# Sixty-four prompt tokens instead of 32 left out of the dense expert products, and two waits moved

## The chip, the cores and the metric

The kernel runs on one core of one Trainium2 chip. The metric is the device time of one execution in microseconds (us). Engines are named as in the profile: PE is TensorE (PEld its weight loads), DVE is VectorE, ACT is ScalarE, POOL is GpSimd, and SP is the engine that only issues DMAs here.

## What is computed

One inference step of a decoder layer, for a prompt of 512 tokens and for 8 sampled tokens, 1024 wide. After an attention and mLSTM part, whose code the change does not touch, comes a layer of single-neuron experts (PEER). Each token has 8 heads, and each head picks 16 of 128 x 128 = 16384 experts:

```python
e = i1[ci // 16] * 128 + i2[ci % 16]              # 8 heads x 16 = 128 experts of each token
g = softmax(sc)                                    # their weights
a = gelu(einsum('td,ted->te', hb, u[e]))           # one dot product for each token and expert
out = einsum('te,ted->td', g * a, v[e])            # weighed sum of the rows of v
```

## The kernel before

The picks are spread over all experts, so the kernel computes most of the layer densely.

**First phase.** For each of 128 chunks of 128 experts (`n` in the code; the table `u` is loaded in groups `g` of four chunks), PE multiplies the table by all 520 tokens: `up(n)`, 32 matmuls of 260 columns (line 2129). Two PSUM pairs alternate, and `up(n)` waits for `gelu(n - 2)` of ACT. ACT applies gelu into `act_f` (line 989) and splits the loaded `u_raw` into `u_g` (line 980); DVE makes the remainder `u_a` (line 1549). SP loads `u` two groups ahead (line 573), and stores the results to HBM: `d_act` for the tokens of the dense part (line 579), `d_acts` for the rest (line 581). Beside the chunks, from n = 45 on, one pair of gates a step turns the picks of 8 dense tokens into dense gate weights: DVE makes one-hot rows, PE multiplies them (line 2150, 16 matmuls), ACT moves them into `stage` (line 997), and SP stores a filled `stage` to `d_gate` (line 585) after every fourth pair. There are NPAIRS pairs.

**Second phase.** For each of the 128 chunks (`q`), PE multiplies the table `v` by the activations times gates: 16 matmuls of DENSE columns (line 2181), the product of a high part (`v_g`, `w_h`) and of a remainder (`v_a`, `w_y`). For each group SP loads `a_in` and `g_in` (`load_weighing`, lines 597 and 598, after DVE has used up the group two before) and 2 MB of `v_raw` (`load_v`, line 591, after PE is done with the group three before). For each chunk ACT makes `v_g` (line 1010) and `w_h` (line 1024), DVE makes `v_a` (line 1722), `w_y` (line 1728) and `w_grown` (line 1715). They may be up to 8 chunks ahead of PE.

**Left out of the dense part.** The last EXTRA prompt tokens and the 8 sampled ones are handled by slots. A slot is 128 pairs of token and expert, one on each partition. POOL gathers one number of `d_acts` for each (`t_dots`, line 792) and one row of `v` of 4 KB for each (`trow`, line 798, 6 buffers, so six slots ahead); DVE weighs four slots' numbers (line 1745) and adds each row times its weight (lines 1749 and 1752) into `s_acc` (sampled tokens, first 8 slots) or `x_acc`. At the end PE sums over the partitions of a token (line 2199). The function `slots_at(q)` says behind which chunk q DVE does which slot, in its own queue, so that a row that has not come holds up DVE.

**The seam of the phases.** The first group of the second phase is prepared while PE is still in the first. SP, in its loop over n, waits at n = AT_FIRST until all gate stores have landed, and then issues the loads of group 0; these and the `u` loads are in one queue. At n = AT_PREPARE and the three steps behind it ACT and DVE prepare its chunks.

Of the kernel before, what the change touches and what calls it, by code (L numbers as in the profile page):

```python
# [34 lines left out]
NG = NKEYS // GC  # L35
TB = 32
LATER = SEQ - P
EXTRA = 32
DENSE = SEQ - EXTRA
NBLK = DENSE // TB  # L40
QUADS = TB // 4
# [6 lines left out]
SSLOTS = DB * H * TOPK // P  # L48
TSLOTS = SSLOTS + EXTRA * H * TOPK // P
BATCH = 4  # L50
LEAD = 6
DOTS = 4
KEPT = EXTRA + DB
SPREAD = P // EXTRA
assert H % SPREAD == 0 and TSLOTS % BATCH == 0 and DENSE % TB == 0
# [7 lines left out]

def slots_at(q):

    return [s for s in range(TSLOTS) if 8 + s * 29 // 10 == q]


COLT = 32
# [5 lines left out]
AT_EXP = 31  # L75
AT_TABLES = 34
AT_GATES = 45
AT_FIRST = 106
AT_PREPARE = 112


def gate_pairs_at(n):
# [78 lines left out]
def trunk_and_peer(nc, I, O):  # L161
# [37 lines left out]
    def put(name, shape, dt, off):  # L199
        return nc.alloc_sbuf_tensor_at(name, shape, dt, offset=off)  # L200
# [23 lines left out]
    t_who = put("t_who", [P, 1], F32, c0 + 4928 + 20 * TSLOTS)  # L224
    xsel = put("xsel", [P, EXTRA], F32, c0 + 8064)
    ones_row = put("ones_row", [H, SEQ], F32, c0)
# [271 lines left out]
    with nc.allow_non_contiguous_dma(reason="a few hundred small elements of the decode batch"), block as blk:  # L498

        @blk.sync  # L500
        def _(sp):
# [81 lines left out]
            def store_gates(n):  # L583
                sp.wait_ge(gl_ev, (n + 1) * QUADS)
                sp.dma_start(d_gate[:, :, GC * TB * n:GC * TB * (n + 1)].rearrange("g p x -> p g x"),
                             stage[n % 2][:, :, :].rearrange("p (g c) t -> p g (c t)", c=GC)).then_inc(g_stored[n % 2], 16)
# [18 lines left out]
            for n in range(NKEYS):  # L605
# [8 lines left out]
                for pair in gate_pairs_at(n):  # L614
                    if pair % (QUADS // 2) == QUADS // 2 - 1:
                        store_gates(pair // (QUADS // 2))
                if n == AT_FIRST:
                    for b in range(2):
# [17 lines left out]
        def _(pool):  # L636
# [146 lines left out]
            for h in range(H):  # L783
                at, s0 = EXTRA * (h % SPREAD), SSLOTS + h // SPREAD * TOPK
                pool.dma_start(t_lists[at:at + EXTRA, :, s0:s0 + TOPK],
# [27 lines left out]
        def _(act):  # L813
# [161 lines left out]
            def u_shrunk(g, s):  # L975
                act.wait_ge(u_in[g % 2][s // 2], 16 * (g // 2 + 1))
                if g >= 2:
                    act.wait_ge(a_made, (g - 1) * GC)
                ks = slice(2 * s, 2 * s + 2)
                A(u_g[g % 2][s // 2][:, 2 * (s % 2):2 * (s % 2) + 2, :], u_raw[g % 2][:, ks, :], ACT.Copy, scale=SHRINK  # L980
                  ).then_inc(ug_done, 1)
# [18 lines left out]
            def v_shrunk(q):  # L1000
                g, c = q // GC, q % GC
                if c == 0:
                    act.wait_ge(v_in[g % VRING], 16 * (g // VRING + 1))
                if q == 0:
                    act.wait_ge(gl_mm, NQUADS)
                if q == GC:
                    act.wait_ge(a_made, NKEYS)
                if q >= VGRING:
                    act.wait_ge(down_used, q - VGRING + 1)
                A(v_g[q % VGRING][:, :], v_raw[g % VRING][:, c, :], ACT.Copy, scale=SHRINK).then_inc(vg_done, 1)  # L1010

            def weights_high(q):
                g, c = q // GC, q % GC
                act.wait_ge(w_made, q + 1)
                if q == 0:
                    for b in range(2):
                        act.wait_ge(g_stored[b], 16 * ((NBLK + 1 - b) // 2))
                if q == GC:
                    for b in range(2):
                        act.wait_ge(a_stored[b], 16 * (NG // 2))  # L1020
                        act.wait_ge(as_stored[b], 16 * (NG // 2))
                if q >= WRING:
                    act.wait_ge(down_used, q - WRING + 1)
                A(w_h[g % 2][:, c, :], w_grown[q % 3][:, :], ACT.Copy, scale=1.0 / GROW).then_inc(wh_done, 1)  # L1024
# [24 lines left out]
            for n in range(NKEYS):  # L1049
# [9 lines left out]
                if n % GC < 2 and 1 <= n // GC < NG - 1:  # L1059
                    for s in (2 * (n % GC), 2 * (n % GC) + 1):  # L1060
                        u_shrunk(n // GC + 1, s)
                if 0 <= n - AT_PREPARE < GC:
                    v_shrunk(n - AT_PREPARE)
                    weights_high(n - AT_PREPARE)
            for q in range(GC, CHUNKS):
# [4 lines left out]
        def _(v):  # L1070
# [475 lines left out]
            def u_rest(g, s):  # L1546
                v.wait_ge(ug_done, g * 4 + s + 1)
                ks = slice(2 * s, 2 * s + 2)
                tt(u_a[g % 2][:, ks, :], u_raw[g % 2][:, ks, :],  # L1549
                   u_g[g % 2][s // 2][:, 2 * (s % 2):2 * (s % 2) + 2, :].bitcast(F32), ALU.subtract).then_inc(ulow_done, 1)  # L1550
# [168 lines left out]
            def v_rest(q):  # L1719
                g, c = q // GC, q % GC  # L1720
                v.wait_ge(vg_done, q + 1)
                tt(v_a[g % VRING][:, c, :], v_raw[g % VRING][:, c, :], v_g[q % VGRING][:, :].bitcast(F32), ALU.subtract  # L1722
                   ).then_inc(vlow_done, 1)
# [7 lines left out]
            def down_step(q):  # L1731
                if 0 <= q - 1 < CHUNKS:
                    v_rest(q - 1)
                if 0 <= q - 2 < CHUNKS:
                    weights_rest(q - 2)
                if q < CHUNKS:
                    weights_grown(q)
# [17 lines left out]
            for n in range((FIRST_LOOPED - 1) * GC, NKEYS):  # L1755
                for pair in gate_pairs_at(n):
                    gate_rows(pair)
                if n % GC == GC - 1 and n // GC + 1 < NG:
                    for s in range(4):
                        u_rest(n // GC + 1, s)  # L1760
                if 0 <= n - AT_PREPARE < GC:
                    down_step(n - AT_PREPARE)
                if n == AT_PREPARE + GC:
                    v_rest(GC - 1)
# [5 lines left out]
            for q in range(GC + 2, CHUNKS + 2):  # L1770
                down_step(q)
                for s in slots_at(q):
                    slot_row(s)
# [538 lines left out]
```

## Time and profile before

| | us |
|---|---|
| Median of 3 runs | 1540.96 (1540.72 to 1545.38) |
| The profiled execution | 1541.64 |
| Its span, first to last instruction | 1539.7 |
| First phase on PE | 513.5 to 1079.1 |
| Second phase on PE | 1079.2 to about 1536 |

PE is busy for 98% of the span, DVE 73%, ACT 39%, POOL 23%. Of the chain of work that ended last, lines 2129 and 2181 are 29% and 28%. The DMA engines are busy 8 to 10 tenths of the time in the second phase up to about 1480 us. Times below count from the start of the span.

### The profile page before, as it was taken

Reading aid. Unit: us, or ns where it says so; the run is one execution under the profiler, and the core shown is the slowest. Engines: PE = TensorE matmul, PEld = TensorE weight load, DVE = VectorE, ACT = ScalarE, POOL = GpSimd, SP = SyncE. Lnnn points to the kernel's source line nnn. Section 1 sums busy time; section 2 is a strip of 40 time slices with the busy share of each in tenths; the row PEclk is TensorE's granted clock in tenths of the full one; section 3 lists DMA queues with packets and bytes.
Section 4 is the critical chain, followed back from the end, with each engine's and each line's share of the span. In section 5 each row is a group of like instructions: output and inputs, shape, how many; then the busy total and the mean of one; then the engine's idle time right before and its main releaser. Section 6 shows DMA issues by size and latency. Waiting matters only on the chain.

```text
span 1539.7 us, 25005 instructions
## 1 busy us (share of the span) xinstructions
PE 1507.4 (98%) x9760; PEld 1288.7 (84%) x9760; DVE 1122.4 (73%) x2475; ACT 601.2 (39%) x992; POOL 347.5 (23%) x369
## 2 busy tenths in 40 slices
PE   9999999999999999999999999979899999999999
PEld 7834445788888999999999999979788888888888
DVE  8739885674999899667777777242488877777773
ACT  2012126600233434535555555343344444444441
POOL 0100213502156576110000000000654533331000
PEclk9999999999999999999999999989999999999999
DMA  5243562404211356667888888866899999889861
GB/s 199 102 109 119 160 221 83 166 4 160 88 55 56 130 173 215 199 211 234 275 278 276 275 279 276 297 231 239 337 387 409 361 346 362 334 340 352 322 266 56
DMA packets 141717, 345.66 MB, mean 225 GB/s; under 512 B 25304, under 2 KB 103408, under 8 KB 127008
## 3 DMA queue, kind: packets, MB, share of 16 engines
q1 hardware_dynamic: 131344, 316.33, 57.8%
q0 software_dynamic: 9968, 27.66, 5.1%
q8 instruction: 78, 1.28, 0.3%
q14 instruction: 39, 0.32, 0.1%
q10 hardware_dynamic: 288, 0.07, 0.0%
HBM read 270.63 MB, written 73.35 MB: 223 GB/s over the span
## 4 chain that ended last, share of the span: by engine, by line
PE 84%; DVE 9%; DMA 4%; ACT 1%; issue 1%; POOL 1%; SPq 0%; DVEq 0%; ACTq 0%; POOLq 0%
PE psum L2129 29%; PE psum L2181 28%; PE psum L1790 20%; PE psum L2150 4%; DMA qrow<-d_q 1%; DMA u_raw<-in_uT 1%; DMA d_gate<-stage 1%; DMA trow<-in_v,t_lists 1%; PE psum L1932 1%; POOL t_dots L792 1%; PE psum L2011 1%; DVE u_a L1549 1%; PE psum L1796 0%; DVE kprod L1216 0%; PE psum L1950 0%
## 5 line engine op out<-in xcount | busy, mean ns | idle before, releaser
L2129 PE MATMUL psum<-h_h,u_g 128*128 128x260 f32 x2048 | 419.0, 286 | 12.6 <-ACT act_f L989 9.9
L2129 PE MATMUL psum<-h_y,u_a 128*128 128x260 f32 x2048 | 410.4, 282 | 0.0
L2181 PE MATMUL psum<-w_h,v_g 128*128 128x480 f32 x1024 | 390.6, 381 | 6.1 <-DVE w_y L1728 6.1
L2181 PE MATMUL psum<-w_y,v_a 128*128 128x480 f32 x1024 | 389.5, 380 | 0.0
L2129 PEld LDWEIGHTS psum<-h_h,u_g 128*128 128x128 f32 x2048 | 315.2, 189 | 13.6 <-ACT act_f L989 10.1
L2129 PEld LDWEIGHTS psum<-h_y,u_a 128*128 128x128 f32 x2048 | 316.4, 189 | 0.0
L1549 DVE TENSOR_TENSOR u_a<-u_raw,u_g 128x1024 fp32r<-128x1024 f32 x128 | 151.2, 1225 | 143.1 <-ACT u_g L980 143.1
L1722 DVE TENSOR_TENSOR v_a<-v_raw,v_g 128x1024 fp32r<-128x1024 f32 x128 | 156.2, 1220 | 99.0 <-ACT v_g L1010 99.0
L2181 PEld LDWEIGHTS psum<-w_h,v_g 128*128 128x128 f32 x1024 | 193.1, 189 | 37.0 <-DVE v_a L1722 6.4
L2181 PEld LDWEIGHTS psum<-w_y,v_a 128*128 128x128 f32 x1024 | 193.1, 189 | 30.1
L1010 ACT ACTIVATE v_g<-v_raw 128x1024 fp32r<-128x1024 f32 x128 | 134.3, 1049 | 122.3 <-DMA v_raw<-in_v 122.3
L989 ACT ACTIVATE act_f<-psum 128x520 f32<-128x520 f32 x128 | 77.4, 605 | 265.6 <-PE psum L2129 265.6
L1790 PE MATMUL psum<-hT,wr 128*128 128x260 f32 x768 | 169.9, 383 | 0.0
L1790 PEld LDWEIGHTS psum<-hT,wr 128*128 128x128 f32 x768 | 145.4, 190 | 22.4 <-DMA wr<-in_w 0.4
L792 POOL DMA_INDIRECT t_dots<-d_acts,t_lists x40 | 56.8, 1421 | 433.5 <-DMA d_acts<-act_f 421.6
L980 ACT ACTIVATE u_g<-u_raw 128x1024 fp32r<-128x1024 f32 x128 | 128.5, 1059 | 28.6 <-DMA u_raw<-in_uT 28.5
L1790 PE MATMUL psum<-wr,hT 128*128 128x512 f32 x304 | 132.4, 593 | 0.0
L798 POOL DMA_INDIRECT trow<-in_v,t_lists x40 | 85.6, 2139 | 188.8 <-DVE x_acc L1752 155.9
L1024 ACT ACTIVATE w_h<-w_grown 128x480 fp32r<-128x480 f32 x128 | 77.1, 602 | 117.7 <-DVE w_grown L1715 114.4
L1790 PEld LDWEIGHTS psum<-wr,hT 128*128 128x128 f32 x304 | 57.0, 190 | 69.3 <-issue 69.3
L1715 DVE SCALAR_TENSOR_TENSOR w_grown<-a_in,g_in 128x480 f32<-128x480 f32 x128 | 83.4, 652 | 15.6 <-DMA g_in<-d_gate 15.5
L1728 DVE SCALAR_TENSOR_TENSOR w_y<-w_h,w_grown 128x480 fp32r<-128x480 f32 x128 | 83.2, 651 | 0.0
(399 smaller groups left out, 1693.6 us busy)
## 6 DMA issues: line engine op xcount, KB each, us to landing
u_raw<-in_uT SPq DMA_DIRECT2D x64, 1024.0 KB, 7.5
v_raw<-in_v SPq DMA_DIRECT2D x32, 2048.0 KB, 8.5
d_act<-act_f SPq DMA_DIRECT2D x32, 960.0 KB, 11.4
d_gate<-stage SPq DMA_DIRECT2D x15, 2048.0 KB, 12.0
a_in<-d_act SPq DMA_DIRECT2D x32, 960.0 KB, 7.4
g_in<-d_gate SPq DMA_DIRECT2D x32, 960.0 KB, 10.1
wr<-in_w SPq DMA_DIRECT2D x13, 2048.0 KB, 8.1
kv<-in_ck SPq DMA_DIRECT2D x24, 256.0 KB, 8.3
```

The source lines that it names most:

```text
L798: pool.indirect_dma_start(trow[s % TROWS][:, :], None, v_rows, bass.IndirectOffsetOnAxis(ap=t_vrow[:, s:s + 1], axis=0)).then_inc(t_row_in ...
L980: A(u_g[g % 2][s // 2][:, 2 * (s % 2):2 * (s % 2) + 2, :], u_raw[g % 2][:, ks, :], ACT.Copy, scale=SHRINK).then_inc(ug_done, 1)
L989: A(act_f[g % 2][:, c, :], upair[n % 2], ACT.Gelu).then_inc(a_gelu, 1)
L1010: A(v_g[q % VGRING][:, :], v_raw[g % VRING][:, c, :], ACT.Copy, scale=SHRINK).then_inc(vg_done, 1)
L1024: A(w_h[g % 2][:, c, :], w_grown[q % 3][:, :], ACT.Copy, scale=1.0 / GROW).then_inc(wh_done, 1)
L1549: tt(u_a[g % 2][:, ks, :], u_raw[g % 2][:, ks, :], u_g[g % 2][s // 2][:, 2 * (s % 2):2 * (s % 2) + 2, :].bitcast(F32), ALU.subtract).then_ ...
L1715: stt(w_grown[q % 3][:, :].rearrange("p (a t) -> p a t", a=NBLK), a_in[g % 2][:, c, :].rearrange("p (a t) -> p a t", a=NBLK), GROW, g_in[g ...
L1722: tt(v_a[g % VRING][:, c, :], v_raw[g % VRING][:, c, :], v_g[q % VGRING][:, :].bitcast(F32), ALU.subtract).then_inc(vlow_done, 1)
L1728: stt(w_y[g % 2][:, c, :], w_h[g % 2][:, c, :].bitcast(F32), 1.0 - GROW, w_grown[q % 3][:, :], ALU.mult, ALU.add).then_inc(wy_done, 1)
L1790: mm = pe.matmul(dst, l, r, start=(n == 0), stop=(n == len(pairs) - 1))
L2129: mm = pe.matmul(upair[n % 2][:, cols], w, hs[:, k, cols], start=(k == 0 and x == 0), stop=(k == KT - 1 and x == 1))
L2181: mm = pe.matmul(ybank[m][:, 0:DENSE], w, z[g % 2][:, c, :], start=(q == 0 and x == 0), stop=(last and x == 1))
```

## The change

```diff
-EXTRA = 32
+EXTRA = 64
 DENSE = SEQ - EXTRA
 NBLK = DENSE // TB
 QUADS = TB // 4
...
 def slots_at(q):
-    return [s for s in range(TSLOTS) if 8 + s * 29 // 10 == q]
+    return [s for s in range(TSLOTS) if 16 + s * 3 // 2 == q]
...
-AT_FIRST = 106
-AT_PREPARE = 112
+AT_FIRST = 109
+AT_PREPARE = 115
```

Everything else follows from these numbers: DENSE goes from 480 to 448, the gate pairs from 60 to 56 and their stores from 15 to 14, the slots from 40 to 72, SPREAD (partitions a token of the prompt has in a slot) from 4 to 2, KEPT (columns of `d_acts`) from 40 to 72. Slots stood behind chunks 8 to 121, one each 2.9 chunks; now they stand behind chunks 16 to 122, two for each three chunks.

SP's queue around the loads of group 0. Before (`v_raw_250`, `a_in_264` and `g_in_266` are the buffers of group 0, the `u_raw` behind them is group 28's):

```order
L573 DMA u_raw_228<-in_uT 128x2048 x2
L579 DMA d_act<-act_f_236 512x1x480
L581 DMA d_acts<-act_f_236 128x4x40
L585 DMA d_gate<-stage_244 128x32x128
L591 DMA v_raw_250<-in_v 128x4096
L597 DMA a_in_264<-d_act 128x1920
L598 DMA g_in_266<-d_gate 128x1920
L573 DMA u_raw_227<-in_uT 128x2048 x2
```

and now:

```order
L585 DMA d_gate<-stage_245 128x32x128
L573 DMA u_raw_228<-in_uT 128x2048 x2
L579 DMA d_act<-act_f_236 512x1x448
L581 DMA d_acts<-act_f_236 128x4x72
L573 DMA u_raw_227<-in_uT 128x2048 x2
L579 DMA d_act<-act_f_235 512x1x448
L581 DMA d_acts<-act_f_235 128x4x72
L591 DMA v_raw_250<-in_v 128x4096
L597 DMA a_in_264<-d_act 128x1792
L598 DMA g_in_266<-d_gate 128x1792
L573 DMA u_raw_228<-in_uT 128x2048 x2
```

The loads of group 0 move from ahead of the `u_raw` load of group 28 to behind it, and there is a whole group between the last gate store and them.

DVE's queue around the first slot. Before, behind `w_grown` of chunk 8 (the `v_a` rows are of chunks 6, 7 and 8):

```order
L1722 TENSOR_TENSOR v_a_254<-v_raw_251,v_g_262 128x1024
L1728 SCALAR_TENSOR_TENSOR w_y_274<-w_h_272,w_grown_270 128x480
L1715 SCALAR_TENSOR_TENSOR w_grown_269<-a_in_265,g_in_267 128x480
L1722 TENSOR_TENSOR v_a_254<-v_raw_251,v_g_263 128x1024
L1728 SCALAR_TENSOR_TENSOR w_y_274<-w_h_272,w_grown_268 128x480
L1715 SCALAR_TENSOR_TENSOR w_grown_270<-a_in_264,g_in_266 128x480
L1745 TENSOR_TENSOR t_wts<-t_dots,t_lists 128x4
L1749 TENSOR_SCALAR s_acc<-trow_275,t_wts 128x1024
L1722 TENSOR_TENSOR v_a_255<-v_raw_252,v_g_256 128x1024
L1728 SCALAR_TENSOR_TENSOR w_y_274<-w_h_272,w_grown_269 128x480
```

and now, behind `w_grown` of chunk 16:

```order
L1715 SCALAR_TENSOR_TENSOR w_grown_269<-a_in_264,g_in_266 128x448
L1745 TENSOR_TENSOR t_wts<-t_dots,t_lists 128x4
L1749 TENSOR_SCALAR s_acc<-trow_275,t_wts 128x1024
L1722 TENSOR_TENSOR v_a_254<-v_raw_251,v_g_256 128x1024
L1728 SCALAR_TENSOR_TENSOR w_y_274<-w_h_272,w_grown_268 128x448
L1715 SCALAR_TENSOR_TENSOR w_grown_270<-a_in_264,g_in_266 128x448
L1752 SCALAR_TENSOR_TENSOR s_acc<-trow_276,t_wts,s_acc 128x1024
L1722 TENSOR_TENSOR v_a_254<-v_raw_251,v_g_257 128x1024
L1728 SCALAR_TENSOR_TENSOR w_y_273<-w_h_271,w_grown_269 128x448
L1715 SCALAR_TENSOR_TENSOR w_grown_268<-a_in_264,g_in_266 128x448
L1722 TENSOR_TENSOR v_a_254<-v_raw_251,v_g_258 128x1024
L1728 SCALAR_TENSOR_TENSOR w_y_273<-w_h_271,w_grown_270 128x448
```

The first slot stood ahead of the `w_y` of chunk 7 (the last row of the first piece); now it stands eight chunks further on, and the second follows after one chunk instead of after two.

## Rows read from the trace of the kernel before

**Rows 1.** The page: span, then an engine's busy time (share) and instructions.
```profile
span 1539.7 us, 25005 instructions
PE 1507.4 (98%) x9760; PEld 1288.7 (84%) x9760; DVE 1122.4 (73%) x2475; ACT 601.2 (39%) x992; POOL 347.5 (23%) x369
```
**Rows 2.** Timeline, ACT: start, duration, engine, line, operation, operands, [idle before <-releaser].
```profile
972.59 0.61 ACT L989 ACTIVATE act_f<-psum 128x520 f32<-128x520 f32 x1 [3.21 <-PE psum L2129]
...
977.39 0.60 ACT L989 ACTIVATE act_f<-psum 128x520 f32<-128x520 f32 x1 [3.21 <-PE psum L2129]
...
1071.69 0.61 ACT L989 ACTIVATE act_f<-psum 128x520 f32<-128x520 f32 x1 [3.23 <-PE psum L2129]
1075.52 0.61 ACT L989 ACTIVATE act_f<-psum 128x520 f32<-128x520 f32 x1 [3.23 <-PE psum L2129]
```
**Rows 3.** Timeline, PE, second phase, two matmuls 50 apart.
```profile
1300.04 0.37 PE L2181 MATMUL psum<-w_y,v_a 128*128 128x480 f32 x1
...
1310.92 0.38 PE L2181 MATMUL psum<-w_y,v_a 128*128 128x480 f32 x1
```
**Rows 4.** Timeline, ACT and SP, around the loads of group 0.
```profile
989.85 0.61 ACT L989 ACTIVATE act_f<-psum 128x520 f32<-128x520 f32 x1 [3.23 <-PE psum L2129]
...
990.87 0.35 SPq L591 DMA_DIRECT2D v_raw<-in_v  x1
...
992.21 1.08 SPq L573 DMA_DIRECT2D u_raw<-in_uT  x2
...
1008.64 2.00 ACT L980 ACTIVATE u_g<-u_raw 128x1024 fp32r<-128x1024 f32 x2 [14.36 <-DMA u_raw<-in_uT]
```
**Rows 5.** Timeline, PE, behind that stall; ten rows of two matmuls apart.
```profile
1011.19 0.80 PE L2129 MATMUL psum<-h_h,u_g 128*128 128x260 f32 x2 [9.88 <-ACT act_f L989]
...
1015.60 0.41 PE L2129 MATMUL psum<-h_h,u_g 128*128 128x260 f32 x2
```
**Rows 6.** Timeline, POOL and DVE, the first gathers and the first slot.
```profile
1086.00 1.06 POOL L792 DMA_INDIRECT t_dots<-d_acts,t_lists  x1 [421.57 <-DMA d_acts<-act_f]
...
1098.24 0.16 DVE L1745 TENSOR_TENSOR t_wts<-t_dots,t_lists 128x4 f32<-128x4 f32 x1 [4.52 <-DMA t_dots<-d_acts,t_lists]
1107.07 0.75 DVE L1749 TENSOR_SCALAR s_acc<-trow,t_wts 128x1024 f32<-128x1024 f32 x1 [8.66 <-DMA trow<-in_v,t_lists]
```
**Rows 7.** Timeline, PE, behind the second stall; 12 matmuls apart.
```profile
1109.67 0.74 PE L2181 MATMUL psum<-w_h,v_g 128*128 128x480 f32 x1 [6.06 <-DVE w_y L1728]
...
1114.55 0.38 PE L2181 MATMUL psum<-w_h,v_g 128*128 128x480 f32 x1
```
**Rows 8.** Timeline, DVE, working without a gap.
```profile
1112.28 1.28 DVE L1752 SCALAR_TENSOR_TENSOR s_acc<-trow,t_wts,s_acc 128x1024 f32<-128x1024 f32 x1
1113.48 1.22 DVE L1722 TENSOR_TENSOR v_a<-v_raw,v_g 128x1024 fp32r<-128x1024 f32 x1
...
1115.75 1.22 DVE L1722 TENSOR_TENSOR v_a<-v_raw,v_g 128x1024 fp32r<-128x1024 f32 x1
```
**Rows 9.** Windows: stretch, length, busy by engine, PE clock, DMA share, GB/s.
```profile
1160.00:1200.00 40.00, 40.00 (x187) 34.59 (x185) 30.53 (x40) 17.30 (x23) 14.36 (x8) 1.00 1.00 409
```
**Rows 10.** DMA queues, 1130 to 1170 us: packets, MB, share of the 16 engines.
```profile
q1 hardware_dynamic: 1453, 13.27, 82.0%
q0 software_dynamic: 880, 2.62, 16.5%
```
**Rows 11.** Timeline, SP's load of group 8, and DVE's first use of it.
```profile
1171.38 0.33 SPq L591 DMA_DIRECT2D v_raw<-in_v  x1
...
1181.87 1.23 DVE L1722 TENSOR_TENSOR v_a<-v_raw,v_g 128x1024 fp32r<-128x1024 f32 x1 [2.91 <-ACT v_g L1010]
```
**Rows 12.** Groups of POOL's instructions, 1120 to 1440 us: busy, mean ns | idle before.
```profile
L798 POOL DMA_INDIRECT trow<-in_v,t_lists x32 | 76.0, 2375 | 186.4 <-DVE x_acc L1752 155.9 <-DVE s_acc L1752 23.6 <-DVE x_acc L1749 6.0
L792 POOL DMA_INDIRECT t_dots<-d_acts,t_lists x27 | 40.7, 1508 | 8.2 <-issue 8.2
```
**Rows 13.** Timeline, POOL: one request made while DVE ran without a gap.
```profile
1206.99 7.71 POOL L792 DMA_INDIRECT t_dots<-d_acts,t_lists  x1 [0.31 <-issue]
```

## The prediction

> **What bounds the kernel now.** I read the page first: PE is busy 1507 of 1539.7 us [rows 1], so time can be gained by fewer columns on PE or by taking its few waits away, and lost by whatever supplies PE. Next come the timelines at both ends of the first phase's last part, for the pace of a step: gelu rows are 4.80 us apart where a gate pair lies in the step and 3.83 us where none does [rows 2], which is 0.1197 us for each of 32 matmuls of 260 columns. In the second phase 50 matmuls of 480 columns take 10.88 us, 0.2176 us each, 3.48 us a chunk [rows 3]. Then the waits of PE. Only two are longer than 3 us, one at the seam (9.88 us, rows 5) and one early in the second phase (6.06 us, rows 7). Last, the suppliers in the second phase: DVE [rows 8], the DMA engines [rows 9, 10] and POOL [rows 12, 13].
>
> **Fewer columns.** 2048 matmuls lose 32 of 480 columns. Between 260 and 480 columns the pace rises by 0.2176 - 0.1197 = 0.0979 us for 220 columns, 0.445 ns a column, so 14.2 ns a matmul and 29.1 us in all. In proportion to the columns it would be 29.7 us. The granted clock is 1.00 there [rows 9], the upper of the two levels (2.4 GHz); one column each cycle of it would be 13.3 ns and 27.3 us. I take 29.1. The chunk becomes 16 x 0.2034 = 3.25 us.
>
> **Fewer gates.** Four steps lose their gate pair: 4 x (4.80 - 3.83) = 3.9 us, since PE works through these steps without a wait. What ACT and DVE save there is beside PE and is worth nothing.
>
> **The stall at the seam.** SP's wait for the last gate store ended at 990.87, and it issued 4 MB for group 0 right then; only behind them, at 992.21, came the `u_raw` load of group 28. The products that this load waits for had ended at 989.85, when the gelu of step 107 began, so the load was ready to go but stood behind the wait and the 4 MB. ACT, whose next work is `u_g` of that group, stood still for 14.36 us until 1008.64 [rows 4], the gelus behind it were late, and PE lost 9.88 us. Then it ran at half clock: 20 matmuls took 1015.60 - 1011.19 = 4.41 us [rows 5] in place of 2.39, 2.0 us more. The whole costs 11.9 us. In the new order the `u_raw` load of group 28 is ahead, and the last gate store is a group earlier, so SP waits for nothing at n = 109. What is late next is the `u_raw` of group 29, issued four steps (15.3 us) after group 28's. Ahead of it in the queue are 2.1 MB of `u`, 1.1 MB of stores, 2.1 MB of `v` and 1.8 MB of `a_in` and `g_in`: 7.1 MB, 17.4 us at 409 GB/s [rows 9]. It meets a backlog of about 2 us, its first half lands some 5 us later, and PE would feel it only beyond about 9 us (two steps and the gelu's turn, less ACT's 2.0 us for that half). I take no stall; the bound is 3 us. Preparing group 0 at n = 115 has over 15 us from its loads, so it waits for none of them. For PE this is 11.9 us less.
>
> **The stall at the first slot.** DVE stood in slot 0 for 4.52 and 8.66 us, because POOL could begin its gathers only at 1086.00, when the last `d_acts` had landed; the `w_y` of chunk 7 stands behind it [rows 6], and PE waited for it. After 6.06 us of idle time 12 matmuls took 4.88 us [rows 7] in place of 2.61: 2.3 us more at the lower clock, 8.3 in all. Now DVE comes to slot 0 behind chunk 16, which it can't reach before group 4's `v` is there, well over 20 us later, when six rows have long landed. What is late next is the `v` of group 3: it is issued when PE ends group 0, 39 - 13 = 26 us before PE wants it; even with 14 us for landing and 3 for ACT and DVE, 9 us are left. 8.3 us less.
>
> **Added work on PE.** The eight sums of `x_acc` get 64 columns in place of 32, and run at most at twice their time. I take 0.5 us more.
>
> **The sum for PE alone.** 29.1 + 3.9 + 11.9 + 8.3 - 0.5 = 52.7 us. From the profiled execution's own 1541.64 us (0.7 above the median of the three runs) this gives 1488.9 us.
>
> **Can the suppliers keep up?** Slots stand behind chunks 16 to 122, 106 chunks or 345 us at PE's new pace; 72 slots, of which 6 rows are there at the start.
> DVE: a chunk takes 2.27 us and a row 1.20 us when it runs without a gap [rows 8]. With 64 of 1984 columns fewer the chunk is 2.20, two thirds of a row 0.80, the weights 0.03: 3.03 of 3.25 us. It keeps up, with 7% to spare.
> The DMA engines: queue q1 moved 13.27 MB in 82.0% of 40 us, 405 GB/s, and q0 2.62 MB of rows and their gathers in 16.5%, 397 GB/s [rows 10]. A chunk now needs 0.983 MB of q1 (2.43 us) and two thirds of 0.524 MB of q0 (0.88 us): 3.31 us against PE's 3.25. That is short by 6 us over 106 chunks, and the reload of `xT` (2.1 MB, 5 us) adds to it: 11 us. By 409 GB/s for all of it [rows 9] it is 6 us; by a rate 5% lower than q1's, as where the queue is not full, 29. Against it stands the lead: the `v` of a group is issued 26 us before PE wants it, was with DVE after 10.5 us [rows 11], and needs about 3 more, so 13 us of lateness cost nothing. So PE loses nothing at 6 or 11 us, and about 16 plus some clock, 20, at 29. I take 3 us, near the lower end, since the full stretch is the nearer row.
> POOL: a row request takes 2375 ns on average and a gather 1508 [rows 12], with two gaps of 0.3 us 4.5 us a slot, of the 4.88 that a slot now has.
>
> On this the Trainium skill (SBUF — State Buffer, Summary: rules for kernel authors) says to reckon with about 358 GB/s between HBM and SBUF. By it a chunk's 1.333 MB would take 3.72 us, 50 us more than PE needs over 106 chunks, and the time would be about 1489 + 50 - 13 = 1526 us. The trace disagrees: 409 GB/s over 40 us.
>
> **Forecast: 1492 us**, 52.7 us gained and 3 lost. Its own range is 1486 to 1497.
>
> **Rivals.**
> 1. The DMA engines become the bound of the second phase. For it: they are already at share 1.00 in a stretch with one slot each 2.9 chunks [rows 9]. Against it: the lead, and 30 of the 128 chunks have no slot. 11 to 29 us short with part of the lead lost and the clock halved after stalls: 1498 to 1512, middle 1503.
> 2. The row supply makes it slower than before. POOL's requests share time with DVE: one took 7.71 us while DVE ran without a gap [rows 13]. DVE now has 7% of gaps in place of 20%. If every row request were of that kind (7.71 + 1.51 + 0.6 = 9.8 us a slot) 66 slots would take 648 us; if half were, with the mean for the others, 7.1 us a slot and 471 us, 126 more than 345; the six rows ahead give back about 18, and PE loses 108: 1597. The point from which the change is slower is (345 + 18 + 53) / 66 = 6.3 us a slot. Against it: a DVE that waits for a row leaves POOL the gap it needs, so it can hardly last.
> The Trainium skill (SBUF — State Buffer, Who interferes with whom) says that a DVE instruction with two SBUF inputs holds a port that GpSimd's reads need, for its whole length. All of DVE's instructions of this stretch are of that kind; the trace agrees in part, most requests getting through in the middle of DVE's run.
> 3. The seam keeps a stall: group 29's load is late, or group 3 of the second phase is. 4 to 10 us with the clock: 1496 to 1502.
> 4. Nothing of the two stalls goes, so only columns and gates count: 1541.6 - 32.5 + 3 = 1512.
>
> **How the numbers follow.** Forecast 0.55, rival 1 0.24, rival 2 0.05 at 1545 or more, rival 3 0.09, rival 4 0.02, milder lateness of rows, 1512 to 1535, 0.03; 0.02 for a gain below 1483. For 8 in 10 the range is 1483 to 1518: it holds the forecast, rivals 1, 3 and 4, with some room above rival 1's end for more than one supplier being late at once, and leaves out the rest. A measurement of this kernel tells 0.3% (4.6 us) from no change. Faster by more than that: 0.94; within it 0.01; slower 0.05.
>
> **What would show it.** PE's row spacing in the second phase: 0.203 us. No wait of PE over 1 us between steps 108 and 128, and the `u_raw` issue ahead of `v_raw`; no wait at chunk 7, and `t_wts` with no idle time before it. DMA share 0.97 to 1.00 from chunk 16 on, the loads of `v` landing after 11 to 18 us, and PE still without idle time. It is wrong if PE's waits for `w_y` or `v_a` come back in the middle of the second phase, with the clock below 1.00: behind a `trow` that came late it is rival 2, behind `v_raw` or `g_in` rival 1.

## The result, and the profile after

| | us |
|---|---|
| Before, median | 1540.97 |
| Changed, median of 4 runs | 1491.69 (1489.78 to 1494.14) |
| Ratio | 0.9675, 95% interval 0.9652 to 0.9697 |
| The profiled execution of the changed kernel | 1489.78 |
| Its span | 1488.0 |

The time fell by 49.3 us; the forecast was 1492. The page of the changed kernel answers to [rows 1]. PE is busy for 36 us less and now for 99% of the span, DVE does 22 us more, POOL 103 us more. Its last row says how much the engines of the DMA moved in each of 40 slices of 37 us: in slices 30 to 38 it stands at 405 to 417.

```profile
span 1488.0 us, 24983 instructions
...
PE 1471.1 (99%) x9696; PEld 1281.1 (86%) x9696; DVE 1144.4 (77%) x2499; ACT 594.5 (40%) x984; POOL 450.9 (30%) x433
...
GB/s 206 76 109 140 106 276 115 172 1 89 122 99 65 58 171 177 231 194 187 274 279 284 284 282 275 273 290 261 286 412 405 408 413 417 414 416 411 409 397 93
```

**The pace.** Two matmuls of the second phase, 50 apart, on PE's timeline, as in [rows 3]. They start 10.16 us apart, so 0.2032 us each; before it was 0.2176.

```profile
1250.01 0.36 PE L2181 MATMUL psum<-w_y,v_a 128*128 128x448 f32 x1
...
1260.17 0.36 PE L2181 MATMUL psum<-w_y,v_a 128*128 128x448 f32 x1
```

**What PE still waits for** after 500 us, in the view of waits (us in total, times, longest). The first row is the start of the first phase. Behind it there is one wait of 0.9 us; before there were waits of 9.88 and 6.06 us [rows 5, 7].

```profile
PE psum L2129 <- DVE u_a L1549: 2.6, 1, 2.6
PE psum L2181 <- DVE w_y L1728: 0.9, 1, 0.9
```

**The gates.** Four steps had a pair of gates before and have none now. Over them the gelus of ACT, which follow PE's steps, come in 15.34 us in place of 19.17: 3.8 us less. Before, on ACT's timeline:

```profile
963.01 0.60 ACT L989 ACTIVATE act_f<-psum 128x520 f32<-128x520 f32 x1 [1.31 <-PE psum L2129]
...
982.18 0.61 ACT L989 ACTIVATE act_f<-psum 128x520 f32<-128x520 f32 x1 [1.31 <-PE psum L2129]
```

and now, the same steps:

```profile
962.56 0.61 ACT L989 ACTIVATE act_f<-psum 128x520 f32<-128x520 f32 x1 [1.31 <-PE psum L2129]
...
977.90 0.61 ACT L989 ACTIVATE act_f<-psum 128x520 f32<-128x520 f32 x1 [0.53 <-PE psum L2129]
```

**The seam**, on the timelines of SP's queue and of ACT, answering to [rows 4]. The last gate store goes out at 959.38. The `u_raw` load of group 28 is issued at 985.56, right when the products of its buffer have ended, ahead of `v_raw` (988.00); `u_g` starts 5.0 us later after 0.57 us of idle time, in place of 14.36. Group 29's load follows at 1000.89. ACT waits for `u_raw` eight times between 960 and 1064 us, 4.3 us at the longest, and none of it shows as a wait of PE. A small loss is left that the view of waits does not list: from 1029 to 1037 us PE gets through 63 matmuls, where a stretch of 8 us at its usual pace has 69. The kernel before has it too (63 matmuls from 1030 to 1038), so it is no part of what the change won.

```profile
959.38 0.38 SPq L585 DMA_DIRECT2D d_gate<-stage  x1
...
985.56 0.80 SPq L573 DMA_DIRECT2D u_raw<-in_uT  x2
...
988.00 0.56 SPq L591 DMA_DIRECT2D v_raw<-in_v  x1
...
1000.89 0.81 SPq L573 DMA_DIRECT2D u_raw<-in_uT  x2
```
```profile
990.57 2.01 ACT L980 ACTIVATE u_g<-u_raw 128x1024 fp32r<-128x1024 f32 x2 [0.57 <-DMA u_raw<-in_uT]
```
```profile
ACT u_g L980 <- DMA u_raw<-in_uT: 8.0, 8, 4.3
```

**The first slot**, on the timelines of POOL and DVE, answering to [rows 6]. POOL makes its first gather at 1069.55. DVE comes to slot 0 at 1099.61, 30 us later, and stands for neither the numbers nor the row. The idle time in front of the next row is a wait for `v_g` of the next group; DVE is well ahead of PE there, and PE doesn't wait.

```profile
1069.55 1.06 POOL L792 DMA_INDIRECT t_dots<-d_acts,t_lists  x1 [404.94 <-DMA d_acts<-act_f]
```
```profile
1099.61 0.16 DVE L1745 TENSOR_TENSOR t_wts<-t_dots,t_lists 128x4 f32<-128x4 f32 x1
1099.81 0.75 DVE L1749 TENSOR_SCALAR s_acc<-trow,t_wts 128x1024 f32<-128x1024 f32 x1
1105.70 1.23 DVE L1722 TENSOR_TENSOR v_a<-v_raw,v_g 128x1024 fp32r<-128x1024 f32 x1 [5.13 <-ACT v_g L1010]
```

**The second phase**, in the view of windows with the columns of [rows 9]. PE has no gap at all, DVE is busy 94%, and the DMA engines are at a share of 1.01 and 413 GB/s. The six windows of 40 us from 1180 to 1420 all read 409 to 416. Below it the queues from 1140 to 1420 us, as in [rows 10]: 115.3 MB in 280 us. And the issues (KB each, median us to landing): the 2 MB of `v` take 15.5 us to land.

```profile
1260.00:1300.00 40.00, 40.00 (x198) 36.94 (x197) 37.66 (x48) 19.07 (x25) 29.87 (x17) 1.00 1.01 413
```
```profile
q1 hardware_dynamic: 9249, 84.98, 73.0%
q0 software_dynamic: 10080, 30.32, 28.1%
...
v_raw<-in_v SPq DMA_DIRECT2D x22, 2048.0 KB, 15.5
...
xT<-d_x SPq DMA_DIRECT2D x1, 2080.0 KB, 20.8
```

The one wait that is left stands behind a load of `v`. The chain that ended last passes from PE to a load of `v` that landed after 20.66 us, from there over `v_g` and `w_y` to PE again. This load was issued while the reload of `xT` was under way (issued at 1141.87, 20.8 us to landing, the row above). The wait is 0.94 us long, and behind it PE runs to the end: apart from the last sums there is nothing else in the chain.

```profile
1099.96 54.49 PE psum L2181 x268
...
1154.47 20.66 DMA v_raw<-in_v
...
1175.15 1.07 ACT v_g L1010
...
1177.39 0.63 DVE w_y L1728
...
1178.15 291.70 PE psum L2181 x1432
```

**POOL**, its groups from 1140 to 1420 us, as in [rows 12].

```profile
L798 POOL DMA_INDIRECT trow<-in_v,t_lists x57 | 97.6, 1712 | 83.9 <-DVE x_acc L1752 76.0 <-issue 7.9
L792 POOL DMA_INDIRECT t_dots<-d_acts,t_lists x53 | 84.9, 1602 | 16.1 <-issue 16.1
```

A row request now takes 1712 ns on average, less than the 2375 of before, though DVE is busier. With two gaps of 0.3 us a slot is 3.9 us of POOL's time, and it waits 76 us for DVE to give a row buffer back: the supply of rows is ahead of DVE, not behind it.

### The profile page after: what moved, and what is told of

Read it like the earlier page. It is cut to its first block, busy times and chain, and to the rows that moved or that the text cites. A ratio compares the mean times of both kernels' runs of the same rounds, so it can differ in the third digit from the quotient of the medians.

```text
span 1488.0 us, 24983 instructions
## 1 busy us (share of the span) xinstructions
PE 1471.1 (99%) x9696; PEld 1281.1 (86%) x9696; DVE 1144.4 (77%) x2499; ACT 594.5 (40%) x984; POOL 450.9 (30%) x433
## 4 chain that ended last, share of the span: by engine, by line
PE 86%; DVE 9%; DMA 3%; ACT 1%; issue 1%; SPq 0%; DVEq 0%; ACTq 0%
PE psum L2129 31%; PE psum L2181 27%; PE psum L1790 21%; PE psum L2150 4%; DMA v_raw<-in_v 1%; DMA qrow<-d_q 1%; PE psum L1932 1%; PE psum L2011 1%; DVE u_a L1549 1%; PE psum L1796 0%; DVE kprod L1216 0%; PE psum L1950 0%; DVE sSc L1217 0%; PE psum L1849 0%; PE psum L1901 0%
## 5 line engine op out<-in xcount | busy, mean ns | idle before, releaser
L2181 PE MATMUL psum<-w_h,v_g 128*128 128x448 f32 x1024 | 376.0, 367 | 0.9 <-DVE w_y L1728 0.9
L2181 PE MATMUL psum<-w_y,v_a 128*128 128x448 f32 x1024 | 373.8, 365 | 0.0
L792 POOL DMA_INDIRECT t_dots<-d_acts,t_lists x72 | 112.4, 1562 | 426.6 <-DMA d_acts<-act_f 404.9
L798 POOL DMA_INDIRECT trow<-in_v,t_lists x72 | 131.1, 1820 | 96.4 <-DVE x_acc L1752 78.5
L1024 ACT ACTIVATE w_h<-w_grown 128x448 fp32r<-128x448 f32 x128 | 73.6, 575 | 122.9 <-DVE w_grown L1715 118.7
L1715 DVE SCALAR_TENSOR_TENSOR w_grown<-a_in,g_in 128x448 f32<-128x448 f32 x128 | 79.6, 622 | 14.2 <-DMA g_in<-d_gate 14.2
L1752 DVE SCALAR_TENSOR_TENSOR x_acc<-trow,t_wts,x_acc 128x1024 f32<-128x1024 f32 x63 | 80.8, 1283 | 0.5
```

What stands on the lines that cost most here:

```text
L792: pool.indirect_dma_start(t_dots[:, s:s + 1], None, d_acts, bass.IndirectOffsetOnAxis(ap=t_arow[:, s:s + 1], axis=0)).then_inc(t_dots_in[b ...
L798: pool.indirect_dma_start(trow[s % TROWS][:, :], None, v_rows, bass.IndirectOffsetOnAxis(ap=t_vrow[:, s:s + 1], axis=0)).then_inc(t_row_in ...
L1715: stt(w_grown[q % 3][:, :].rearrange("p (a t) -> p a t", a=NBLK), a_in[g % 2][:, c, :].rearrange("p (a t) -> p a t", a=NBLK), GROW, g_in[g ...
L1752: ins = stt(acc[:, :], trow[s % TROWS][:, :], t_wts[:, s:s + 1], acc[:, :], ALU.mult, ALU.add)
L2181: mm = pe.matmul(ybank[m][:, 0:DENSE], w, z[g % 2][:, c, :], start=(q == 0 and x == 0), stop=(last and x == 1))
```

## The experiments

The theory after the result was that of the prediction: fewer columns and gates, both stalls gone, and a second phase whose DMA engines are full but whose lead hides it. Three things in it were not shown by the two traces. Which of the edits took which stall away? What does the full DMA cost? And how far is each supplier from being the bound?

**e1: the waits alone, on the kernel before.**

```diff
-AT_FIRST = 106
-AT_PREPARE = 112
+AT_FIRST = 109
+AT_PREPARE = 115
```

> The kernel before (32 tokens left out, slots as before) with only the two waits moved, from steps 106 and 112 to 109 and 115. Theory: the stall at the seam, 9.88 us idle and 2.0 us at the lower clock, comes from the u load of group 28 standing behind the loads of group 0. Here it stands ahead of them, so the stall goes: 1541 - 11.9 = 1529 us, with no wait of PE over 3 us between 980 and 1070 us. Rival: the last gate store (issued at 979) still fills the queue when the u load is issued, or the u load of group 29 is late instead; then half or more of the stall stays: 1535 to 1541 us.

Measured: 1531.3 us (1529.28 to 1535.8), ratio 0.993 (0.9909 to 0.9952), beside a median of 1541.78 on that chip: 10.5 us less. The load of `u_raw` (995.07) is ahead of `v_raw` now, and of PE's waits after 900 us the one at the seam is gone, but for 0.3 us; that of the first slot stands.

```profile
PE psum L2181 <- DVE w_y L1728: 6.2, 1, 6.2
PE psum L2129 <- ACT act_f L989: 0.3, 1, 0.3
```

The stall is worth 10.5 us by the medians, where the prediction had 11.9; the interval (7 to 14 us off) holds both. The traces tell it more closely. From the gelu at 977.39 to the one at 1075.52 [rows 2] the kernel before takes 98.13 us, and e1 takes 86.66 us over the same 22 steps, so 11.5 us less. What blurs the medians lies elsewhere: in e1's profiled execution the first phase began on PE at 517.5 us in place of 513.5, far ahead of anything that the edit touches.

```profile
982.62 0.60 ACT L989 ACTIVATE act_f<-psum 128x520 f32<-128x520 f32 x1 [3.21 <-PE psum L2129]
...
1069.28 0.61 ACT L989 ACTIVATE act_f<-psum 128x520 f32<-128x520 f32 x1 [3.23 <-PE psum L2129]
```

**e2: the slots later, alone, on the kernel before.** 40 slots, from chunk 16 on in place of chunk 8.

```diff
-    return [s for s in range(TSLOTS) if 8 + s * 29 // 10 == q]
+    return [s for s in range(TSLOTS) if 16 + s * 27 // 10 == q]
```

> The kernel before with only the slots' places changed: 40 slots from behind chunk 16 to behind chunk 121 in place of 8 to 121. Theory: the wait of PE for the w_y of chunk 7 (6.06 us idle, 2.3 us at the lower clock) is DVE standing in slot 0; with the slot eight chunks later it goes: 1541 - 8.3 = 1532.7 us. Rival: the loads of v for groups 2 and 3 are late at that place anyway, so PE stalls some chunks further on, and the time stays above 1537 us.

Measured: 1533.44 us (1533.13 to 1536.29), ratio 0.9946 (0.9928 to 0.9964): 8.3 us less (6 to 11 by the interval), where the prediction had 8.3. By the traces the second phase on PE is 8.5 us shorter (456.6 to 448.1 us between its first and last `w_y` matmul). This time the wait of the slot is gone, and that of the seam is there, in the same view:

```profile
PE psum L2129 <- ACT act_f L989: 8.6, 1, 8.6
```

So the two stalls are independent, and by the medians 18.8 of the 49.3 us, some 4 us either way, were to be had without leaving out a single token more. The other 30.5 are the columns, the gates and what was added; the prediction had 29.1 + 3.9 - 0.5 - 3 = 29.5 for them.

**e3: the changed kernel with the waits put back** at 106 and 112.

```diff
-AT_FIRST = 109
-AT_PREPARE = 115
+AT_FIRST = 106
+AT_PREPARE = 112
```

> The changed kernel with the two waits put back to steps 106 and 112. Theory: with 64 tokens left out the last gate store is issued four steps earlier and has landed when SP comes to step 106, so SP issues the loads of group 0 at once, a step or more ahead of the u load of group 28, and they are through in time: the moved waits are worth nothing here, 1491.7 us within 2 us. Rival: the order of the queue alone makes the stall (4 MB ahead of the u load): it comes back, and the time is 1500 to 1504 us.

Measured: 1492.11 us (1491.27 to 1492.96), ratio 0.9682 (0.9662 to 0.9703): no difference from the changed kernel. SP's queue shows why. The last gate store goes out at 961.40, a group earlier than at 32 tokens, so the wait at n = 106 is over early. `v_raw` is issued at 975.51, and the `u_raw` that was stuck before is issued at 987.58, 10 us behind the loads of group 0 and with no wait in front of it.

```profile
961.40 0.38 SPq L585 DMA_DIRECT2D d_gate<-stage  x1
...
972.25 1.23 SPq L573 DMA_DIRECT2D u_raw<-in_uT  x2
...
975.51 0.99 SPq L591 DMA_DIRECT2D v_raw<-in_v  x1
...
987.58 0.81 SPq L573 DMA_DIRECT2D u_raw<-in_uT  x2
```
```profile
PE psum L2181 <- DVE w_y L1728: 0.2, 1, 0.2
```

Each of the two edits, the moved waits and the 64 tokens, takes the stall of the seam away by itself. Together they take it away once. In the changed kernel the moved waits are worth nothing that the runs can show.

**e4: the changed kernel with its first slot behind chunk 8 again.**

```diff
-    return [s for s in range(TSLOTS) if 16 + s * 3 // 2 == q]
+    return [s for s in range(TSLOTS) if 8 + s * 8 // 5 == q]
```

> The changed kernel with its 72 slots from behind chunk 8 to behind chunk 121, one each 1.6 chunks, in place of 16 to 122. Theory: DVE comes to slot 0 at about 1077 us, the first row lands at about 1091, and PE wants the w_y of chunk 7 at about 1085.5: 7 us idle and 2.3 us at the lower clock, 1501 us. Rival: the more even spacing (a slot each 1.6 chunks in place of 1.5) relieves the DMA engines by 0.06 us a chunk, and wins back what the stall costs: 1492 to 1495 us.

Measured: 1502.38 us (1500.64 to 1503.94), ratio 0.9743 (0.9722 to 0.9765): 10.7 us more than the changed kernel. The waits of before are back on DVE's timeline (4.52 and 8.66 us in [rows 6]), and PE waits for 6.6 us behind them. The other 1.9 us of the view below come at 1190.75, well behind, at the place where the changed kernel has its 0.9 us. With 64 tokens left out, too, the place of the first slot is what counts.

```profile
1084.81 0.16 DVE L1745 TENSOR_TENSOR t_wts<-t_dots,t_lists 128x4 f32<-128x4 f32 x1 [4.82 <-DMA t_dots<-d_acts,t_lists]
1092.60 0.75 DVE L1749 TENSOR_SCALAR s_acc<-trow,t_wts 128x1024 f32<-128x1024 f32 x1 [7.63 <-DMA trow<-in_v,t_lists]
```
```profile
PE psum L2181 <- DVE w_y L1728: 8.4, 2, 6.6
```

**e9: the slots from chunk 12 on**, so that they are spread over more chunks (one each 1.55 in place of 1.5).

```diff
-    return [s for s in range(TSLOTS) if 16 + s * 3 // 2 == q]
+    return [s for s in range(TSLOTS) if 12 + s * 31 // 20 == q]
```

> The changed kernel with its slots behind chunks 12 to 122, one each 1.55 chunks, in place of 16 to 122 each 1.5. DMA theory: a chunk needs 0.03 us less of the DMA engines, so the 0.9 us wait goes and the time falls by 0 to 1 us. Rival: the first row has not landed when DVE comes to slot 0 at about 1090 us, DVE waits, and PE, which has 9 us in hand for group 3, loses 0 to 3 us: up to 1495.

Measured: 1493.23 us (1492.87 to 1493.88), ratio 0.9686 (0.9671 to 0.97), beside 1492.4 for the changed kernel on the same chip (e10). The time lies where the rival had it, up to 1495, but its wait is not there. DVE does wait for rows at the start, 1.0 us at 1092 and 1.3 at 1105, but PE does not wait behind them. PE's only wait of the phase is the one at the reload of `xT`, and it did not go, as more even slots should have made it: it grew from 0.9 to 2.65 us.

```profile
1181.30 0.44 PE L2181 MATMUL psum<-w_h,v_g 128*128 128x448 f32 x1 [2.65 <-DVE w_y L1728]
```

Chunk 16 is as good a place or better. Why the wait grew was not taken apart.

**e7: the changed kernel with fewer bytes.** From group 2 on, `g_in` is loaded in its first block only, 64 KB in place of 896. What is left out is the true value of the gates there; all the work on the engines stays.

```diff
+                if g < 2:
                     sp.dma_start(g_in[g % 2][:, :, :, :]...
+                else:
+                    sp.dma_start(g_in[g % 2][:, 0, :, :]...
```

> The changed kernel with the same cut of the g_in loads (from group 2 on only the first of 14 blocks is loaded, the other blocks' gates are left old). It takes a fifth of the DMA work of the second phase away and nothing else. If the DMA engines cost the changed kernel the 3 us that the prediction allowed, the time falls from 1491.7 to about 1489; if the lead hides all of it, it stays within 1 us. If anything falls by more than 4 us, the prediction's sum was right only by two errors that cancel.

Measured: 1490.81 us (1490.41 to 1494.44), ratio 0.9673 (0.9652 to 0.9695). From 1180 to 1300 us the share of the DMA engines is down to 0.90 to 0.96, and PE waits for nothing after 900 us, but the time is the same within a microsecond. The bytes moved are a seventh less (354 in place of 413 GB/s, 1130 to 1370 us), not the fifth that was expected. The traces show a small gain that the medians blur: PE's second phase, from its first to its last matmul with `w_y`, takes 421.3 us in the changed kernel and 419.6 in e7. (Lines stand 4 higher in this kernel.)

```profile
L2181 PE MATMUL psum<-w_y,v_a x1024: 360/365/372, 1063.0 to 1484.3; 128*128 128x448 f32 x171
```
```profile
L2185 PE MATMUL psum<-w_y,v_a x1024: 360/365/372, 1065.0 to 1484.6; 128*128 128x448 f32 x171
```

One of the windows of e7, with the columns of [rows 9]:

```profile
1220.00:1260.00 40.00, 40.00 (x199) 36.95 (x198) 35.40 (x46) 18.32 (x25) 24.54 (x16) 1.00 0.90 325
```

**e8: the changed kernel without its 32 added slots.** 40 slots as before; the products are as narrow as in the changed kernel, so 32 slots of pairs are left out of the result. The same 40 stands in POOL's loop and in PE's wait for the rows. **e10** is the changed kernel again, on the same chip.

```diff
-    return [s for s in range(TSLOTS) if 16 + s * 3 // 2 == q]
+    return [s for s in range(40) if 16 + s * 27 // 10 == q]
...
```

> The changed kernel with its dense products of 448 columns, but only 40 of its 72 slots, spaced as in the kernel before, behind chunks 16 to 121; the other 32 slots are left out, so the experts' part of the 64 prompt tokens is incomplete. The difference to the changed kernel is what the 32 added slots cost. If they are hidden but for the 0.9 us wait seen in the profile: 1490 to 1491.5 us. By the prediction's 3 us for supply: 1488.7. If it falls below 1487, the added slots cost PE time that its waits don't show.

> The changed kernel as it is, once more, so that the next two have it on the same chip: 1491.7 us within 2 us.

Measured: e8 1490.4 us (1489.11 to 1491.13), ratio 0.9664 (0.965 to 0.9679); e10 1492.4 us (1490.93 to 1494.59), ratio 0.9679 (0.9662 to 0.9695). The difference is 2.0 us and the intervals overlap. In the traces PE's second phase takes 419.6 us in e8 and 421.1 in e10, so 32 more slots cost 1.5 us. They bring 40 us of work to DVE and 97 to POOL by the pages of the two kernels, beside PE, with the DMA engines at share 0.96 to 0.97 in e8 and at 1.01 in the changed kernel.

e8 also tells the columns: it has as many slots at the same places as e2, and neither has a wait of PE in the second phase, which takes 448.1 us there, 28.5 more.

**e5: a slot behind every chunk from 16 on**, where the changed kernel has two behind each three. This is what rivals 1 and 2 were about, driven further: a chunk now moves 0.983 + 0.524 = 1.507 MB.

```diff
-    return [s for s in range(TSLOTS) if 16 + s * 3 // 2 == q]
+    return [s for s in range(TSLOTS) if 16 + s == q]
```

> The changed kernel with one slot behind each chunk from 16 to 87, in place of two for each three chunks up to 122. The work is the same; the need of a chunk in that stretch grows. DMA theory: 0.983 + 0.524 MB a chunk at the measured 413 GB/s are 3.65 us against PE's 3.25, 29 us short over 72 chunks and 5 for the reload of xT, less 13 us of lead: 20 us more than 1491.7, about 1512, the waits behind v_raw. DVE theory: 2.21 + 1.20 + 0.04 = 3.45 us a chunk, 14 us short, within the lead: 1492 to 1496. POOL theory: 3.9 us a slot in the changed kernel's profile, 47 us short, less 18 of rows ahead: 1520, the waits behind trow.

Measured: 1517.6 us (1517.03 to 1522.54), ratio 0.9838 (0.982 to 0.9856), 25 to 26 us more than the changed kernel. PE waits for `w_y` eleven times, and in the window it gets through 173 matmuls in place of 198, with the DMA engines at share 1.02. DVE stood for a late `trow` nine times, 14.0 us in all. That is what the POOL theory had said, and its 1520 us are nearer than the 1512 of the DMA theory, so the time alone does not tell the two apart; e6 does. The waits of PE, and one window:

```profile
PE psum L2181 <- DVE w_y L1728: 13.6, 11, 3.0
```
```profile
1250.00:1290.00 40.00, 36.71 (x173) 31.33 (x172) 36.83 (x48) 15.97 (x22) 30.59 (x23) 1.00 1.02 414
```

**e6: the same with the bytes of e7.**

> As e5_slot_each_chunk, but from group 2 on the load of g_in brings only the first of its 14 blocks (64 KB in place of 896), so the gates of the other blocks are old ones and their part of the result is left wrong; DVE, ACT, POOL and PE do the same work. DMA theory: a chunk needs 1.30 MB, 3.15 us at 413 GB/s, under PE's 3.25: the waits of e5 go, and the time is 1489 to 1494 us. POOL or DVE theory: the time stays where e5 is, within 4 us.

Measured: 1495.93 us (1492.98 to 1497.54), ratio 0.9692 (0.9672 to 0.9712), 1.9 us above the 1489 to 1494 expected by the DMA theory and far from e5, near which the POOL or DVE theory had it. So 21.7 of the 25.5 us that e5 loses are the DMA engines' doing. POOL makes the same requests in both; what changed is how long a row takes to land, in the middle (1130 to 1370 us), first e5, then e6:

```profile
trow<-in_v,t_lists POOLq DMA_INDIRECT x61, 16.3
```
```profile
trow<-in_v,t_lists POOLq DMA_INDIRECT x59, 9.6
```

What is left, about 4 us, goes with DVE's pace: it is busy for 39.89 of 40 us. The DMA engines are not idle in e6 either (share 0.96 to 1.02 from 1130 to 1330 us), so a part of the 4 us may be theirs. DVE's timeline shows one chunk with its row, 3.40 us from `v_a` to `v_a`, and PE's first matmul of a chunk comes in the same 3.40 us, in place of 3.25. (Lines stand 4 higher here, too.)

```profile
1250.00:1290.00 40.00, 39.67 (x187) 33.82 (x186) 39.89 (x51) 17.32 (x23) 32.99 (x24) 1.00 0.97 375
```
```profile
1291.45 1.23 DVE L1726 TENSOR_TENSOR v_a<-v_raw,v_g 128x1024 fp32r<-128x1024 f32 x1
...
1293.66 1.29 DVE L1756 SCALAR_TENSOR_TENSOR x_acc<-trow,t_wts,x_acc 128x1024 f32<-128x1024 f32 x1
1294.85 1.23 DVE L1726 TENSOR_TENSOR v_a<-v_raw,v_g 128x1024 fp32r<-128x1024 f32 x1
```

The 1512 us expected of e5 were 5.6 too few. A likely reason, which no run took apart: the sum behind it had the DMA shortage alone. In e5 DVE needs its 3.40 us a chunk as well, so it can't make up the lead that a late load has cost, and after a stall PE goes on at DVE's pace, not at its own (184 matmuls in 40 us from 1210 on, where the changed kernel has 198). Not all of the 25.5 us were put to single rows: the waits listed are 13.6 us, and PE's weight loads stood 12.1 us more, 41 times, at starts of chunks (9.9 us, 33 times, in e6).

Of the kernels here that leave nothing out, the changed one, e3 and e9 lie within 2 us of one another, and none is clearly faster than the changed one.

## Why the prediction was right, and where it was off

**Columns: right.** It had 0.2034 us a matmul and 3.25 us a chunk, the trace shows 0.2032. The spacing fell by 0.2176 - 0.2032 = 14.4 ns a matmul, 29.5 us over 2048. That speaks for the line between 260 and 480 columns (14.2 ns) against one column each cycle (13.3 ns), and does not tell the line from plain proportion (14.5). The pair e2 and e8 gives 28.5 us for the whole phase, with the added sums taken off, so 29.1 lies between the two measurements. The added sums themselves came to some 0.2 us (0.17 in place of 0.14 us, eight times, in the chains), where 0.5 was taken.

**Gates: right.** 3.8 us over the four steps, where the prediction had 3.9.

**Seam: right in size, half right in its cause.** It named two reasons for the stall to go, the new order and the store that is a group earlier, and costed them as one. e3 shows that the second is enough. e1 gives the first 10.5 us by the medians and 11.5 by the traces, where 11.9 was taken. That group 29's load would be next, and harmless, came true with little to spare: issued at 1000.89, its first half was with ACT at 1009.6 after a wait of 4.3 us, 8.7 us later, where the prediction put the bound at about 9.

**First slot: right.** 8.3 us predicted, 8.3 in e2. The 10.7 of e4 hold 0.9 us more of the wait at the reload of `xT`. Six rows were said to have landed long before slot 0. Six were asked for, the first at 1079.63 us and the sixth at 1097.55, so the last ones were still under way; slot 0 takes the first, and it didn't matter. e9, with slot 0 four chunks earlier, shows the margin: there DVE had to wait 1.0 us and took the first row at 1092.06, where the changed kernel takes it at 1099.81.

**Supply: the mechanism right, its size too large.** It had the DMA engines short by 6 to 11 us and a lead of 13 us against it, by which its own sum is a loss of nothing; the 3 us it took were a choice between that and the 20 of the slower rate, not a sum. Shares of 1.01 and landings of 15.5 us for `v` (predicted 0.97 to 1.00 and 11 to 18) say that it read the state of the engines rightly. The rate was the term that was off: 405 and 397 GB/s by the two queues' shares of one stretch of 40 us, where both together moved 413 over 280 us. At 413 a chunk's 1.333 MB take 3.23 us, and nothing is short but for `xT`. The cost is 0.9 us of wait in the trace, and 1.7 us of the second phase by e7 and 1.5 by e8.

On this the Trainium skill (SBUF — State Buffer, Summary: rules for kernel authors) has about 358 GB/s between HBM and SBUF, which gave 1526 us. The runs disagree with it: 413 GB/s over 280 us, and 1491.7 us.

**Rival 1** (the DMA engines as the bound) did not come, but e5 shows that it is real and how near: one slot more each three chunks costs 26 us, 22 of them the DMA engines' by e6. **Rival 2** (the supply of rows) was argued from a request of 7.71 us. Such requests still happen, the longest seen between 1238 and 1268 us took 5.31. But they did not become more frequent with DVE's load: over 3 us took 7 of 59 requests before and 4 of 122 now (1120 to 1440 us), and the mean fell. (DVE had gaps of 24% before by [rows 9], not the 20% of the prediction, and has 6% now.) POOL needed 3.9 us a slot, far from the threshold of 6.3. The Trainium skill (SBUF — State Buffer, Who interferes with whom) says that a DVE instruction with two SBUF inputs gets in the way of a GpSimd instruction that reads SBUF. The traces agree in part: in e6, beside a DVE that runs such instructions of 0.6 to 1.3 us without a gap, a request took 1.37 or 1.43 us (rows below), against 0.95 us where DVE stands still (at 1101.01 in the changed kernel). It is held up by less than one of DVE's instructions. Requests of 5 us and more are longer than any of them, and what holds those up no run shows. **Rival 3** (a stall left at the seam) did not come: PE's view of waits has none there. **Rival 4** fell with e1 to e4.

**The sum, and luck.** By the traces, 28.5 for columns and sums, 3.8 for gates, 12.1 for the seam (the last 22 steps, 982.18 to 1079.35 before and 977.90 to 1063.01 now), 8.5 for the slot, less 1.6 for the supply, are 51.3 us. The two profiled executions are 51.9 apart, the medians 49.3. The errors of the terms are within 1 us each but for the supply, so the mechanism was read rightly. That the forecast of 1492 is only 0.3 us off the median is in part luck: the executions of the changed kernel spread from 1489.8 to 1494.1.

Two things stay open: why the wait at the reload of `xT` grew in e9, and how the 4 us that e6 keeps are shared between DVE and the DMA engines. More than 64 tokens left out was not tried: the buffers of the activations would have to be laid out anew.

## What to carry to other kernels

Both stalls here, 19 us together, came from a wait that stood in a queue in front of work that was ready: place a consumer where its supply can have landed, and look at what stands behind each wait. When a change drives a resource to a share of 1.00, that alone says nothing of the time: reckon what is short in all, set it against the lead of the loads, and take the rate from a stretch in which the resource is full. When two edits aim at the same stall, put one back in the result: here one of them was worth nothing any more.

## What the runs showed of the hardware that was not expected

- The DMA engines, with 2 MB loads, 896 KB loads and indirect gathers of 4 KB rows in two queues, moved 409 to 416 GB/s for 280 us on end. In the changed kernel the full state showed as latency (the 2 MB of `v` took 15.5 us to land, 20.8 us for the 2 MB of `xT`) and as 1.5 to 1.7 us of PE's time.
- POOL's indirect requests got shorter on average where DVE got busier: 2375 to 1712 ns for rows while DVE went from 76% (30.53 of 40 us, [rows 9]) to 94%, and 1477 ns in e5. Single ones took from 0.95 to 5.3 us in the same stretch. In e6, where DVE has no gap and repeats itself each 3.40 us, POOL falls in step with it: on its timeline each row request takes 1.36 or 1.37 us and each gather 1.42 or 1.43 (1.63 where DVE weighs four slots' numbers in between). So what a request costs looks like a matter of which of DVE's instructions it meets, not of how busy DVE is; which one makes it 5 us long was not found.

```profile
1277.12 1.43 POOL L796 DMA_INDIRECT t_dots<-d_acts,t_lists  x1 [0.30 <-issue]
1278.86 1.37 POOL L802 DMA_INDIRECT trow<-in_v,t_lists  x1 [0.30 <-issue]
```
